# An opening that also reads x by tokens: row sums on ScalarE, roots as columns, and another order of the first five jobs

## What is computed

```python
def rms_norm(x, g):
    x32 = x.astype(jnp.float32)
    y = x32 * lax.rsqrt(jnp.mean(x32 * x32, axis=-1, keepdims=True) + EPS)
    return (y * g.astype(jnp.float32)).astype(x.dtype)

h = rms_norm(x, norm_g[layer])                    # 2048 x 1024
proj = h @ w_in[layer]                            # 1024 -> 68 tiles of 128 columns
...
kv_mem = rms_norm(mem, mem_norm_g[layer]) @ w_mem_kv[layer]    # 256 tokens, 1024 -> 1024
...                                               # three branches, gates, merge
x = x + merged @ w_out[layer]
return rms_norm(x, final_norm_g)
```

## Time and profile before

| | us |
|---|---|
| median of 3 runs | 2505.06 |
| lowest, highest | 2504.25, 2505.44 |
| the profiled execution | 2503.99 |
| its span in the profile | 2502.2 |
| TensorE busy | 2477.8 |
| VectorE busy | 1407.4 |
| ScalarE busy | 588.6 |
| GpSimd busy | 192.6 |

### The profile page before, as it was taken

One profiled execution on the slowest core, in us unless ns is written; L12 is line 12 of the kernel. 1 busy time (PEld: TensorE's weight loads), 2 busy tenths in 40 slices (PEclk: granted clock), 3 DMA queues, 4 the chain that ended last, 5 costly groups with the idle time before them and its releaser, 6 DMA issues.

```text
span 2502.2 us, 31563 instructions
## 1 busy us (share of the span) xinstructions
PE 2477.8 (99%) x12520; PEld 2005.4 (80%) x12520; DVE 1407.4 (56%) x2586; ACT 588.6 (24%) x1266; POOL 192.6 (8%) x332
## 2 busy tenths in 40 slices
PE   8999999999999999999999999999999999999998
PEld 6788888888887777788777777888888888888887
DVE  5736677576644444422444443444435768787776
ACT  3412222222211111112333343322251112010201
POOL 0000000000001111110000000011110000100000
PEclk9999999999999999999999999999999999999999
DMA  5223434434344445541323344467764765758572
GB/s 195 88 80 86 116 93 123 122 93 115 112 137 134 136 148 171 168 147 59 116 97 122 114 135 138 136 206 237 215 229 167 273 170 179 246 176 243 157 219 71
DMA packets 171990, 373.40 MB, mean 149 GB/s; under 512 B 26943, under 2 KB 72099, under 8 KB 165956
## 3 DMA queue, kind: packets, MB, share of 16 engines
q1 hardware_dynamic: 133540, 224.55, 29.4%
q0 software_dynamic: 35184, 140.55, 16.6%
q10 hardware_dynamic: 3120, 6.29, 0.8%
HBM read 239.86 MB, written 131.43 MB: 148 GB/s over the span
## 4 chain that ended last, share of the span: by engine, by line
PE 96%; DVE 1%; DMA 1%; ACT 1%; issue 0%; POOL 0%; DVEq 0%; SPq 0%; ACTq 0%
PE bank L136 28%; PE bank L138 28%; PE bank L137 28%; PE bank L2091 2%; PE bank L2055 1%; PE bank L1904 1%; PE bank L2112 1%; PE bank L2134 1%; PE bank L2070 1%; PE bank L2009 1%; PE bank L2012 1%; PE bank L1995 1%; DMA xa<-x_t 1%; PE bank L2122 1%; ACT tsc L1108 0%; PE bank L1973 0%
## 5 line engine op out<-in xcount | busy, mean ns | idle before, releaser
L136 PE MATMUL bank<-h_hi,w_hi 128*128 128x512 f32 (+1 forms) x2720 | 1083.2, 398 | 1.7 <-DVE h_lo L1338 0.8
L138 PE MATMUL bank<-h_hi,w_lo 128*128 128x512 f32 (+1 forms) x2720 | 1057.1, 389 | 0.0
L137 PE MATMUL bank<-h_lo,w_hi 128*128 128x512 f32 (+1 forms) x2720 | 1056.9, 389 | 0.0
L136 PEld LDWEIGHTS bank<-h_hi,w_hi 128*128 128x128 f32 x2720 | 510.8, 188 | 118.3 <-issue 13.3
L138 PEld LDWEIGHTS bank<-h_hi,w_lo 128*128 128x128 f32 x2720 | 510.7, 188 | 108.3
L137 PEld LDWEIGHTS bank<-h_lo,w_hi 128*128 128x128 f32 x2720 | 511.2, 188 | 103.0 <-issue 1.7
L128 DVE CAST w_hi<-w_raw 128x1024 fp32r<-128x1024 f32 (+1 forms) x122 | 83.9, 687 | 309.0 <-PE bank L138 291.8
L136 PE MATMUL bank<-h_hi 128*128 128x512 f32 (+1 forms) x464 | 172.3, 371 | 1.1 <-DVE xq L1834 1.1
L138 PE MATMUL bank<-h_hi,h_lo 128*128 128x512 f32 (+1 forms) x464 | 170.4, 367 | 0.0
L137 PE MATMUL bank<-h_lo,h_hi 128*128 128x512 f32 (+1 forms) x464 | 170.4, 367 | 0.0
L890 POOL DMA_DIRECT2D proj_d<-ev x160 | 88.6, 554 | 939.1 <-ACT ev L1068 572.5
(11 more groups left out here) (230 smaller groups left out, 2241.3 us busy)
## 6 DMA issues: line engine op xcount, KB each, us to landing
proj_d<-ev POOLq DMA_DIRECT2D x160, 256.0 KB, 2.8
w_raw<-w_in SPq DMA_DIRECT2D x68, 512.0 KB, 5.1
gt<-proj_d POOLq DMA_DIRECT2D x32, 768.0 KB, 7.8
proj_d<-ev POOLq DMA_DIRECT2D x22, 1024.0 KB, 4.8
w_raw<-w_br SPq DMA_DIRECT2D x32, 512.0 KB, 4.3
wx_raw<-w_br SPq DMA_DIRECT2D x32, 512.0 KB, 4.3
o_d<-ev POOLq DMA_DIRECT2D x12, 1024.0 KB, 6.5
ev<-o_d SPq DMA_DIRECT2D x12, 768.0 KB, 4.3
```

The lines of the kernel that those rows point to most:

```text
L136: nc.tensor.matmul(out, ah, bh, start=(start and n == 0), stop=False)
L137: nc.tensor.matmul(out, ah, bl, start=False, stop=False)
L138: last = nc.tensor.matmul(out, al, bh, start=False, stop=(stop and n == len(pairs) - 1))
```

## The change

x and the memory are given a second time, by tokens: `x_n` and `mem_n`, in pieces of 256 tokens, each 128 partitions by two tokens by 1024 channels (1 MB). There are nine pieces: two for each chunk and one for the memory. ScalarE squares a token's row in one instruction of 128x1024 that also adds the row up (`ss`), so the sums are columns: one number for each token on its partition. The root and the reciprocal are then taken of 128x4 numbers (`rcol`), VectorE multiplies the identity with each column (`diag`, 128x512), and one matmul with the ones matrix (`spread`) puts the four diagonals on all partitions, in a PSUM bank that the scaling reads directly. A root's table is loaded ahead of all work by a dummy root.

The pieces 0 and 1 are the first things on SP's queue; the other seven go over GpSimd's queue, each when the piece two before it has been squared. The transposed x and memory are still loaded, since the products need them. The memory gets a room of its own (`mem_room`, the place of `k_mem` and `v_mem`, which are written later), so that chunk 1's load needs no free buffer, and SP issues it. The jobs are now chunk 0, chunk 1, the memory, chunk 2, chunk 3; the banks and the places of the memory weights change with that.

In the rows below a name is the tile of the program; bank stands for any PSUM bank, L1896 and L1933 are the dummy matmuls, L1904 the sums, L1940 the spread.

The core of the diff; left out are names of semaphores, counts shifted in later stages, the banks in later waits and the preparation of the new inputs:

```diff
-        k_mem = sb(ctx, "k_mem", [P, MH, ML])
-        v_mem = sb(ctx, "v_mem", [P, 2, MH * MD])
+        mem_room = sb(ctx, "mem_room", [P, KD * ML])
+        k_mem = mem_room[:, 0:MH * ML].rearrange("p (h m) -> p h m", h=MH)
+        v_mem = mem_room[:, MH * ML:].rearrange("p (s m) -> p s m", s=2)
...
-        KV_BANK = (1, 5, 6, 7)
+        KV_BANK = (6, 7, 6, 7)
+        SUM_BANK = (2, 3, 2, 3, 2)
+        FIRST_BANK = ((0, 1, 3, 2), (4, 5, 6, 7))
...
-                sq = sb(pn, "sq", [P, KD, CW])
-                rstd = sb(pn, "rstd", [P, 2, CW])
+                xn = sb(pn, "xn", [P, 2, 2, D])
+                diag = sb(pn, "diag", [P, 2, CW // P, P])
+                ss = sb(pn, "ss", [P, 2, CW // P])
+                rcol = sb(pn, "rcol", [P, 2, CW // P])
...
-        xbuf = (xa, xb)
+        mb = mem_room[:, :].rearrange("p (k c) -> p k c", k=KD)
+        xbuf = (xa, xb, mb, xa, xb)
...
-        jobs.insert(1, (ML, mem_t, slice(0, ML), None, 1))
+        jobs.insert(2, (ML, mem_t, slice(0, ML), None, 1))
+        pieces = [x_n[0], x_n[1], x_n[2], x_n[3], mem_n[0], x_n[4], x_n[5], x_n[6], x_n[7]]
+        JOB_PIECES = ((0, 1), (2, 3), (4,), (5, 6), (7, 8))
+        PIECE_DONE = (2, 4, 7, 9, 12, 15, 17, 20, 22)
+        ROOT_DONE = (5, 10, 13, 18, 23)
+        F0 = len(jobs)
...
-                load_x(0, slice(0, KD // 2), x_loaded[0])
-                load_x(0, slice(KD // 2, KD), x_half_loaded)
-                load_pair(sp, 0, w_in[TILES[0][1]], w_in[TILES[1][1]])
+                    sp.dma_start(xbuf[j][:, ks, 0:w], src[:, ks, cols]).then_inc(loaded, 16)
+
+                for p in range(2):
+                    sp.dma_start(xn[:, p, :, :], pieces[p]).then_inc(xn_loaded[p], 16)
                 sp.dma_start(g_in[:, 0, :], norm_g).then_inc(const_loaded, 16)
+                sp.dma_start(ident[:, :], ident_c).then_inc(const_loaded, 16)
                 sp.dma_start(g_in[:, 1, :], mem_norm_g).then_inc(const_loaded, 16)
                 sp.dma_start(g_in[:, 2, :], final_g).then_inc(const_loaded, 16)
                 sp.dma_start(bg[:, :], b_gate).then_inc(const_loaded, 16)
                 sp.dma_start(bglu[:, :], b_glu).then_inc(const_loaded, 16)
-                sp.dma_start(ident[:, :], ident_c).then_inc(const_loaded, 16)
                 sp.dma_start(sign[:, :], sign_c).then_inc(const_loaded, 16)
+                sp.dma_start(w_raw[:, 0, :, :], w_in[TILES[0][1]]).then_inc(w_loaded[0], 16)
+                load_x(0, slice(0, KD // 2), x_loaded[0])
+                load_x(0, slice(KD // 2, KD), x_half_loaded)
+                sp.dma_start(w_raw[:, 1, :, :], w_in[TILES[1][1]]).then_inc(w_loaded[1], 16)
                 load_x(1, slice(0, KD), x_loaded[1])
+                load_x(2, slice(0, KD), yr_loaded[3])
...
+                for p in range(2, len(pieces)):
+                    pool.wait_ge(root_done, PIECE_DONE[p - 2])
+                    pool.dma_start(xn[:, p % 2, :, :], pieces[p]).then_inc(zs_loaded[p % 2], 16)
...
+                nc.scalar.activation(rcol[:, 1, 0:1], eps[:, 0:1], ACT.Sqrt)
+
                 def squares(j):
-                    w = jobs[j][0]
-                    act.wait_ge(x_loaded[j % 2], 16 * (j // 2 + 1))
-                    for k in range(KD):
-                        if j == 0 and k == KD // 2:
-                            act.wait_ge(x_half_loaded, 16)
-                        if j:
-                            act.wait_ge(sq_used, 8 * (j - 1) + k + 1)
-                        nc.scalar.activation(sq[:, k, 0:w], xbuf[j % 2][:, k, 0:w],
-                                             ACT.Square).then_inc(sq_ready, 1)
+                    for i, p in enumerate(JOB_PIECES[j]):
+                        if p < 2:
+                            act.wait_ge(xn_loaded[p], 16)
+                        else:
+                            act.wait_ge(zs_loaded[p % 2], 16 * (p // 2))
+                        for t in range(2):
+                            nc.scalar.activation(xn[:, p % 2, t, :], xn[:, p % 2, t, :], ACT.Square,
+                                                 accum_out=ss[:, j % 2, 2 * i + t:2 * i + t + 1]).then_inc(root_done, 1)
 
                 def root(j):
-                    w = jobs[j][0]
-                    act.wait_ge(sq_used, 8 * (j + 1))
+                    n = jobs[j][0] // P
+                    act.wait_ge(root_done, ROOT_DONE[j] - 1)
                     if j >= 2:
-                        act.wait_ge(scaled, 8 * (j - 1))
-                    nc.scalar.activation(rstd[:, j % 2, 0:w], psum[2 + j % 2][:, 0:w], ACT.Sqrt,
+                        act.wait_ge(f_mm, j - 1)
+                    nc.scalar.activation(rcol[:, j % 2, 0:n], ss[:, j % 2, 0:n], ACT.Sqrt,
                                          bias=eps[:, 0:1], scale=1.0 / D).then_inc(root_done, 1)
...
-                    act.wait_ge(h_ready, 2 * (j - 1))
-                    act.dma_start(xbuf[j % 2][:, :, :], x_t[:, :, jobs[j][2]]).then_inc(x_loaded[j % 2], 16)
+                    act.wait_ge(h_ready, 2 * (j - 2))
+                    act.dma_start(xbuf[j][:, :, :], x_t[:, :, jobs[j][2]]).then_inc(x_loaded[j - 3], 16)
...
                 squares(0)
                 root(0)
+                hi_parts(0)
                 squares(1)
                 root(1)
-                hi_parts(0)
-                load_x(2)
-                hi_parts(1)
-                load_x(3)
                 squares(2)
                 root(2)
+                load_x(3)
+                hi_parts(1)
+                squares(3)
+                root(3)
+                load_x(4)
+                hi_parts(2)
+                squares(4)
+                root(4)
                 keep_kv(0)
                 keep_kv(1)
-                squares(3)
-                hi_parts(2)
-                root(3)
-                load_x(4)
                 keep_kv(2)
+                hi_parts(3)
                 keep_kv(3)
-                squares(4)
-                hi_parts(3)
-                root(4)
                 hi_parts(4)
...
                 def normalised(j):
+                    n = jobs[j][0] // P
+                    dve.wait_ge(root_done, ROOT_DONE[j])
+                    r = rcol[:, j % 2, 0:n]
+                    nc.vector.reciprocal(r, r).then_inc(rstd_done, 1)
+                    dve.wait_ge(rstd_done, 2 * j + 1)
+                    nc.vector.tensor_tensor(diag[:, j % 2, 0:n, :], ident[:, :].unsqueeze(1).to_broadcast((P, n, P)),
+                                            r.unsqueeze(2).to_broadcast((P, n, P)), ALU.mult).then_inc(rstd_done, 1)
+
+                def scaled_parts(j):
                     w, gi = jobs[j][0], jobs[j][4]
-                    dve.wait_ge(root_done, j + 1)
-                    r = rstd[:, j % 2, 0:w]
-                    nc.vector.reciprocal(r, r).then_inc(rstd_done, 1)
-                    dve.wait_ge(rstd_done, j + 1)
-                    x = xbuf[j % 2]
+                    dve.wait_ge(*((x_loaded[0], 16), (x_loaded[1], 16), (yr_loaded[3], 16), (x_loaded[0], 32),
+                                  (x_loaded[1], 32))[j])
+                    dve.wait_ge(f_mm, j + 1)
+                    r = psum[SUM_BANK[j]][:, 0:w]
+                    x = xbuf[j]
                     for k in range(KD):
...
                 split_pair(dve, 0, None, slots=(0,))
+                dve.wait_ge(const_loaded, 112)
+                nc.vector.tensor_scalar(bgh[:, :], bg[:, :], 0.5, None, ALU.mult).then_inc(consts, 1)
                 normalised(0)
+                scaled_parts(0)
+                normalised(1)
                 split_pair(dve, 0, None, slots=(1,))
-                normalised(1)
+                normalised(2)
+                scaled_parts(1)
+                scaled_parts(2)
+                normalised(3)
                 split_kv(0)
                 split_kv(1)
+                normalised(4)
                 split_kv(2)
-                normalised(2)
                 split_kv(3)
-                normalised(3)
-                normalised(4)
+                scaled_parts(3)
+                scaled_parts(4)
...
-                def sum_squares(j):
+                def spread(j):
+                    pe.wait_ge(rstd_done, 2 * j + 2)
+                    if j >= 2:
+                        pe.wait_ge(scaled, 8 * (j - 1))
                     w = jobs[j][0]
-                    if j >= 2:
-                        pe.wait_ge(root_done, j - 1)
-                    for k in range(KD):
-                        pe.wait_ge(sq_ready, 8 * j + k + 1)
-                        nc.tensor.matmul(psum[2 + j % 2][:, 0:w], ones[:, :], sq[:, k, 0:w],
-                                         start=(k == 0), stop=(k == KD - 1)).then_inc(sq_used, 1)
+                    nc.tensor.matmul(psum[SUM_BANK[j]][:, 0:w], ones[:, :],
+                                     diag[:, j % 2, 0:w // P, :].rearrange("p n c -> p (n c)"),
+                                     start=True, stop=True).then_inc(f_mm, 1)
...
-                warm(16)
```

(20 more changed lines are left out.)

56 lines of the change are left out of this document (30 added, 26 removed).

## The result

The changed kernel took 2489.53 us (median of 4 runs, 2488.43 to 2491.45) against 2505.03 for the kernel before beside it: a ratio of 0.9939, 95% interval 0.9922 to 0.9957. It is 15.5 us faster. The profiled execution took 2488.43 with a span of 2486.6, against a span of 2502.2 before.

What follows compares the result with a forecast made beforehand. TensorE, busy 99% of the span, was taken as the bound. `project` would begin at 28.8 + 69.7 + 21.6 = 120.1, 2.6 us before 122.7, giving 2502.5 us, range 2495 to 2510.5.

Steps and rivals of the forecast that it cites:

- P0 + 69.7 + W: Begin of `project`: first product's start (28.8), TensorE work (69.7), all later waiting and slow clock (21.6); 120.1 against 122.7 before.
- At 300 GB/s from 2.0 it lands at 23.7: Opening: chunk 0's second half of x, behind about 6.5 MB of loads, sets the first product's start.
- I take 9: Piece 4, chunk 1's first tokens: its load takes 9 us beside other loads, landing at 39.9; alone 5.2.
- Tile 1: TensorE's wait before tile 1 over chunk 0, for ScalarE's squares, then diagonals and second weight split on VectorE: 1.5 us.
- Chunk 1: TensorE's wait for chunk 1's first low half, behind piece 4: 8.7 us, plus 1.8 of slow clock, together 10.5.
- Memory product 0: Wait before the first memory product, its high half behind chunk 2's squares: 2.9 us plus 1.8 slow clock, 4.7.
- Memory product 1: Wait for the second memory product's weights, landing 8.5 us after issue: 2.8 us plus 1.8 slow clock, 4.6.
- Chunk 2: Wait around memory products 2, 3 and chunk 2, whose first half is ready at 98.4: 0.3 us.
- My rival with free loads: Opening loads don't hinder each other: W about 8.5, `project` at 107; halfway 113.5, 2496 us; chance 0.28, shared with no slow clock.
- GpSimd's issues *are* held up: GpSimd's DMA issues wait for VectorE's casts, pieces 4 and 6 up to 0.7 us later each: 2504; within the 0.57 case.
- The last rival: Change doesn't do as said: clock stays high in gaps (5.4 us, 2497), or ScalarE's summed rows cost half more (2505).
- the loads hold the whole chain: 9.4 MB more on the same engines delays the opening's scalings: `project` at 128.8, 6.1 us later, 2511; chance 0.15.

Runs made afterwards that it cites:

- the diagonals between the scalings: Changed kernel, with VectorE building the memory's diagonals between the fourth and fifth scaling of chunk 1, not ahead of all eight: 2488.55 us.
- both of VectorE's edits: Changed kernel, memory's diagonals built between chunk 1's fourth and fifth scaling, and first memory product's weights split ahead of scaling the memory: 2485.75 us.
- eight spreads: Changed kernel, with eight matmuls where each of the spreads 1 to 4 has one: 2500.17 us.
- the filled gap: Changed kernel, with 22 dummy matmuls in TensorE's wait for chunk 1: 2491.84 us.
- the run with the memory behind: Changed kernel, with the memory's norm, diagonals and spread moved behind chunk 1's work on ScalarE, VectorE and TensorE: 2490.02 us.
- the small pieces: Changed kernel, with GpSimd's seven pieces loading 8 of 1024 columns, 7.3 MB not moved: 2483.73 us.

## Why the prediction was wrong, step by step

The structure held. The form P0 + 69.7 + W gave the result once its terms are the measured ones, the shift at `project` reached the end one to one, the 69.7 us of work were right to the 1.1 left over, the chain ran through the engines I had named, and the largest wait was the one before chunk 1's low half. The sign of the forecast was right too, but to a gain of over 0.2% I gave only 0.28. The miss at `project` is 120.1 - 107.3 = 12.8 us: 1.8 in P0 and 11.0 in W, and most of it lies in how long loads took.

**The step that failed: "At 300 GB/s from 2.0 it lands at 23.7", and with it "I take 9" for piece 4.** The rate came from a stretch that averages a start and a tail with nothing queued (shares of 0.78 and 0.10 above), and I treated this average as what the engines can do; the 343 that I called best held the start, and 422 stood in the same trace. Measured were 352 GB/s from 2 to 8 and 408 from 8 to 28. The 9 us came from 0.5 MB weights behind two 2 MB loads of x, though the earlier trace rows had 5.2 for a load of piece 4's size on its own queue. It took 5.7. That the rate is why the landings were short is not shown: from 29 to 35, while piece 4 was under way, the engines moved 315 GB/s at a share of 0.91, and from 36.9 to 50 290 GB/s, about what I had reckoned with. Fewer other loads may have been left by then, but no run separates this. Shown is that the waits follow the bytes: they shrank without the pieces and grew with 7 MB more. Term by term:

- **P0**: 28.8 forecast, 27.03 measured. x's second half landed at 21.96 and not 23.7, and the dummies ended just before 27.03 and not at 28.3: here TensorE's dummies and the low half ended together, and either of them as I had it would have left P0 at 28.3 or later. The load's part hides two errors. Between 2 and 21.96 the rate was 386 GB/s, at which my 6.5 MB would have landed at 18.8; but 7.7 MB moved in that time, so more ran beside x than I counted. The dummies' part is in some measure luck: the first 48 took 12.35 us here and up to 13.81 in traces whose start is the same program, where the first product then stood at up to 28.02. Such a delay shortens the wait before chunk 1 by as much and need not cost time.
- **Tile 1**: 1.5 forecast, 0.4 measured. The squares were done at 30.8 against 33.3. Of these 2.5 us 1.8 are the earlier x, which moved TensorE as well and so shortens no wait; 0.7 are ScalarE's, whose four rows took 4.3 us and not 5.0. A row began every 1.04 us, with the reading of the accumulator inside that time, where I had added 0.19 to each.
- **Chunk 1**: 10.5 forecast (8.7 and 1.8 of clock), 6.8 measured (5.37 and 1.4). Piece 4 was issued at 29.01 and took 5.7, which is 3.3 of the 3.7:

```profile
xn<-mem_n POOLq DMA_DIRECT2D x1, 1024.0 KB, 5.7
```

  The clock's part was right in kind (0.53 again) and was measured by itself when the gap was filled.
- **Memory product 0**: 4.7 forecast, nothing measured; the largest miss. I had piece 6 issued at 42.4 and landed near 56, with ScalarE's high half of the memory behind its squares. It was issued at 37.20 and ScalarE squared all four rows of chunk 2 without a wait:

```profile
37.20 0.53 POOL L943 DMA_DIRECT2D xn<-x_n  x1 [5.58 <-ACT xn L1032]
```

```profile
45.01 1.04 ACT L1032 ACTIVATE xn<-xn 128x1024 f32<-128x1024 f32 x1
...
49.89 2.01 ACT L1050 ACTIVATE h_hi<-mem_room 128x1024 fp32r<-128x1024 f32 x2 [0.30 <-DVE mem_room L1359]
```

  Five microseconds come from the earlier start, and the landing took under 10 where I had 13.6.
- **Memory product 1**: 4.6 forecast, 2.0 measured, with 6.6 us from the free slot to the weight where I had 8.5, and no low clock behind this wait of 1.99, while behind 2.83 us in the run with the diagonals between the scalings there was one:

```profile
62.68 0.69 DVE L129 CAST h_hi<-w_raw 128x1024 fp32r<-128x1024 f32 x1 [4.79 <-DMA w_raw<-w_kv]
```

- **Chunk 2**: 0.3 forecast and 0.3 measured. Against all this stand the 1.1 us left over.

The low clock alone is 4.0 of the 12.8: I had charged 1.8 three times, and 1.4 came once, since the waits behind which I put the other two shrank or were gone.

The waits follow each other, so one early landing pays at each of them, and nearly every term erred to the same side. That is why a sum of cautious terms is not a cautious sum. The range failed for the same reason. My rival with free loads had its full form at W 8.5 and 107, and the measured values are 10.6 and 107.3; the two points agree more closely than the two W because P0 was 1.8 earlier than I had it, which is luck. But the range went only to the rival's halfway point, as if its parts were independent.

The 2 MB loads of x did get in the way: they took 12.5 and 13.6 us, no less than before. The rival was right on the small loads beside them, not on these.

GpSimd's issues *are* held up by VectorE's casts, as that rival had it, but this cost almost nothing. In the changed kernel only piece 3 was issued beside a cast (10.67, cast from 10.45): it took 0.59 us and ended 0.12 behind the cast's end. With both of VectorE's edits piece 7 met one (timelines of GpSimd and VectorE):

```profile
44.60 0.81 POOL L943 DMA_DIRECT2D xn<-x_n  x1 [7.11 <-ACT xn L1032]
```

```profile
44.60 0.68 DVE L129 CAST h_hi<-w_raw 128x1024 fp32r<-128x1024 f32 x1
```

That issue took 0.81 us and again ended 0.13 behind the cast; the pieces 4 and 6, which the rival needed, met none and took 0.53. The last rival had two halves and neither came: the clock did drop (1.4 us), and ScalarE's rows cost a little less than assumed. That the loads hold the whole chain needed 7 MB more.

What stays open is how many GB/s a full share stands for. From 3 to 5 the kernel before moved 316 at 0.98, with x by channels first, and the changed kernel 422 at 1.01, with the pieces first; from 7 to 9 they moved 419 at 1.05 and 311 at 1.06. Short runs in the pieces didn't bring it down much (394). And landings differ by a microsecond or more between executions (piece 4 took 5.6 to 7.1 us in runs where nothing ahead of it had been changed), so half a microsecond between two versions, as with the diagonals between the scalings, is not explained by their traces.

## What to carry to other kernels

Take the rate of a load from a stretch in which the engines are kept supplied, leave out the start, and look at the share beside the GB/s before calling an average a capacity; where terms of a sum hang on one rate, vary them together, from end to end. A statistic that is computed off the busiest engine can be worth more than the work it saves there, since everything that waits for it is freed from that engine's order. When a wait is taken away and the time doesn't move, read the next wait on the same chain before giving up: here taking both gave what taking the first didn't.

## What was new about the hardware

- With SP's and GpSimd's loads under way the DMA engines moved 408 GB/s from 8 to 28 us at a share of 1.04, and 406 when 7 MB more were asked for. The kernel before had 343 from 2 to 8, but 389 to 422 in single microseconds from 5 to 10.
- A load of 1 MB from GpSimd's queue (piece 4) landed in 5.7 us, and a load of 2 MB that ScalarE issued 8 us later took 12.5; both are about as long as in the kernel before, although much more was under way around them. It isn't so for all: the first two pieces on GpSimd's queue took 10.0 us (median), and the other four 6.7.
- A DMA issue on GpSimd took 0.53 to 0.70 us, and cut in four it took 2.88 us: the issue itself is worth counting where an engine hands out many small loads.
- An issue on GpSimd that a VectorE cast of 128x1024 ran beside ended 0.12 to 0.13 us behind the cast's end: 0.59 us in the changed kernel, 0.93 with eight spreads, 0.91 with the filled gap, 0.81 and 1.05 with both of VectorE's edits. In the run with the memory behind, where the cast began at 11.01 and the issue at 10.67, it took 0.55 and wasn't held.
- After an idle time of 5.37 us TensorE was granted 0.53 of its clock, about 1.2 GHz, over the next 3 us; behind 2.48 us, with both of VectorE's edits, it was 0.67 over 3.6 us; behind 2.83 us, with the diagonals between the scalings, 0.50 over 3 us; behind 1.99 us in the changed kernel and 1.90 us with the small pieces it stayed at the upper level.
